# The second half of the adaLN product moves from TensorE to GpSimd

## What is computed

```python
c_act = jax.nn.silu(c)
mod = (c_act @ ada_w[l] + ada_b[l])[:, None, :]          # ada_w: 1024 x 6144
shift1, scale1, gate1, shift2, scale2, gate2 = jnp.split(mod, 6, axis=-1)
u = x * (1.0 + scale1) + shift1
q, k, v, lru_x, lru_gate, gate_a, gate_b = jnp.split(u @ w_in[l], split_at, axis=-1)
...                                                       # attention, RG-LRU, gates -> y
x = _layer_norm(ALPHA * x + gate1 * (y @ w_out[l]), ln1_g[l], ln1_b[l])
u = x * (1.0 + scale2) + shift2
f = _grouped_moe(u, router_w, router_b, moe_w_gate[l], moe_w_up[l], moe_w_down[l])
x = _layer_norm(ALPHA * x + gate2 * f, ln2_g[l], ln2_b[l])
```

## Time and profile before

| | |
|---|---|
| median of three runs | 703.65 us (700.12 to 706.14) |
| profiled execution, time | 704.6 us |
| profiled execution, span of its instructions | 702.8 us |
| mean granted TensorE clock | 0.972 |
| busy: PE, DVE, ACT, POOL | 643.3, 386.0, 221.7, 77.7 us |
| instructions | 15620 |

### The profile page before, as it was taken

One profiled execution on the slowest core, in us unless ns is written; L12 is line 12 of the kernel. 1 busy time (PEld: TensorE's weight loads), 2 busy tenths in 40 slices (PEclk: granted clock), 3 DMA queues, 4 the chain that ended last, 5 costly groups with the idle time before them and its releaser, 6 DMA issues.

```text
span 702.8 us, 15620 instructions
## 1 busy us (share of the span) xinstructions
PE 643.3 (92%) x6021; PEld 433.1 (62%) x6022; DVE 386.0 (55%) x769; ACT 221.7 (32%) x452; POOL 77.7 (11%) x135
## 2 busy tenths in 40 slices
PE   3889999999999899999999956779999999999884
PEld 0377565677777777777778744445555555556363
DVE  0182544367689886466657548653444334433356
ACT  0162533377855565455540142000000000000031
POOL 0032001000000000000000001211122112221400
PEclk9999999999999999999999956999999999999998
DMA  9979976532245342222489794999999999999942
GB/s 322 376 233 329 308 243 216 205 94 87 62 150 165 129 148 81 70 61 91 134 320 419 260 412 162 379 418 398 376 420 417 420 420 417 421 420 420 415 174 120
DMA packets 83070, 188.20 MB, mean 268 GB/s; under 512 B 7084, under 2 KB 59404, under 8 KB 67672
## 3 DMA queue, kind: packets, MB, share of 16 engines
q1 hardware_dynamic: 67808, 148.72, 56.4%
q0 software_dynamic: 7184, 31.74, 12.2%
q10 hardware_dynamic: 8040, 7.23, 3.0%
HBM read 174.12 MB, written 13.54 MB: 267 GB/s over the span
## 4 chain that ended last, share of the span: by engine, by line
PE 78%; DVE 8%; issue 5%; ACT 5%; DMA 3%; SPq 0%; DVEq 0%; ACTq 0%; PEldq 0%
PE psum L1666 22%; PE psum L1676 10%; PE psum L1466 9%; PE psum L1467 8%; PE psum L1468 8%; DMA ada<-in_ada_w_dram 3%; PE psum L1423 3%; PE psum L1587 2%; PE psum L1588 2%; PE psum L1589 2%; PE psum L1712 2%; PE psum L1509 1%; PE psum L1537 1%; PE psum L1547 1%; PE psum L1521 1%
## 5 line engine op out<-in xcount | busy, mean ns | idle before, releaser
L1666 PE MATMUL psum<-wu,xs 128*32 128x256 f32 x1280 | 151.1, 384 | 5.2 <-issue 5.1
L1466 PE MATMUL psum<-uh,whi 128*128 128x512 f32 x336 | 137.7, 410 | 0.0
L1467 PE MATMUL psum<-ul,whi 128*128 128x512 f32 x336 | 131.6, 392 | 0.0
L1468 PE MATMUL psum<-uh,wlo 128*128 128x512 f32 x336 | 131.5, 391 | 0.0
L1666 PE MATMUL psum<-wg,xs 128*32 128x256 f32 x864 | 99.1, 380 | 5.9 <-issue 3.4
L957 DVE TENSOR_TENSOR wlo<-raw,whi 128x1024 fp32r<-128x1024 f32 x42 | 51.3, 1223 | 65.1 <-ACT whi L690 64.8
L882 ACT ACTIVATE hsil<-psum 64x256 f32<-64x256 f32 x40 | 15.0, 376 | 225.7 <-PE psum L1666 225.7
L1283 DVE STREAM_TRANSPOSE xs<-xring 128x256 f32<-128x256 f32 x40 | 26.3, 658 | 106.3 <-PE psum L1666 106.2
L1666 PEld LDWEIGHTS psum<-wg,xs 128*32 128x32 f32 x864 | 51.6, 110 | 47.2 <-issue 18.3
L1676 PE MATMUL psum<-wd,hT 128*32 128x256 f32 x1280 | 78.5, 379 | 2.1 <-DVE hT L1321 1.1
L1666 PEld LDWEIGHTS psum<-wu,xs 128*32 128x32 f32 x1280 | 72.3, 111 | 10.8 <-issue 10.1
(11 more groups left out here) (285 smaller groups left out, 807.0 us busy)
## 6 DMA issues: line engine op xcount, KB each, us to landing
wu<-in_moe_w_up_dram SPq DMA_DIRECT2D x32, 1024.0 KB
wd<-in_moe_w_down_dram SPq DMA_DIRECT2D x32, 1024.0 KB
wg<-in_moe_w_gate_dram SPq DMA_DIRECT2D x22, 1024.0 KB
raw<-in_w_in_dram SPq DMA_DIRECT2D x42, 512.0 KB, 4.1
ada<-in_ada_w_dram POOLq DMA_DIRECT2D x16, 1024.0 KB, 6.7
wg_later<-in_moe_w_gate_dram SPq DMA_DIRECT2D x10, 1024.0 KB
ada<-in_ada_w_dram SPq DMA_DIRECT2D x8, 1024.0 KB, 15.2
y_d<-ysb ACTq DMA_DIRECT2D x144, 32.0 KB
```

Of the source, the lines that this page charges most:

```text
L1466: mmul(bank[s % 2], h[:, k, :], uh[:, k, :], start=(k == 0), stop=False)
L1467: mmul(bank[s % 2], h[:, k, :], ul[:, k, :], start=False, stop=False)
L1468: ins = mmul(bank[s % 2], l[:, k, :], uh[:, k, :], start=False, stop=(k == KT - 1))
L1666: ins = mmul(psum[32 * g:32 * g + 32, 0, 0:256].rearrange("p (a m) -> p a m", a=2), xs[:, k, :], w[:, g % 2], start=(k == 0), stop=(k == K ...
```

## The change

The 4096 columns of the second half are cut into 32 pieces of 128 x 1024 (512 KB), four for each of the eight sets of rows. GpSimd loads them into three buffers of half the former size, multiplies each with its column of silu(c) and adds it to a sum `part2` (128 x 4096) in SBUF. That is one instruction for each of the first four pieces and two for each of the other 28: 60 in all. It does this at steps 1 to 16 (20 pieces) and 25 to 33 (12 pieces), each released by `proj_ps`, the count of finished tiles. After tile 34 and after tile 35 PE adds up the 128 partitions by four products with ones each, in bank 7, and DVE's seven instructions follow at its steps 35 and 36. GpSimd, and no longer SyncE, stores the eight rows to `mod_d`; the waits in SyncE's queue are gone. The loads of `adab2` and `ln1row` move to steps 31 and 32, `zrow` is zeroed first of all, and its nine stores stand behind the pieces of the same step.

```diff
-NA2 = 16
+NA2 = 32
 A2_BUFS = 3
-A2_AT = [3 + (10 * n) // NA2 for n in range(NA2)]
+A2_STEP = [1 + (4 * n) // 5 for n in range(20)] + [25 + (3 * n) // 4 for n in range(12)]
+MOD2_STEP = 34
...
                 if t == START[4] - 3:
-                    sp.wait_ge(S["mod2_row"], 2)
                     load_bias(1)
...
-                if t == 17:
-                    for h in range(2):
-                        sp.wait_ge(S["mod2_row"], h + 1)
-                        for g in range(4):
-                            sp.dma_start(mod_d[h, g:g + 1, :], mod2row[32 * g:32 * g + 1, h, :]).then_inc(mod2_out, 16)
...
+            def load_ada2(n):
+
+                if n >= A2_BUFS:
+                    pool.wait_ge(S["ada2_used"], 2 * (n - A2_BUFS + 1))
+                if n < NA2:
+                    pool.dma_start(ada2[n % A2_BUFS][:, :], ada_v[:, n // 4, (2 + n % 4) * D:(3 + n % 4) * D])\
+                        .then_inc(ada2_sem[n % A2_BUFS], 16)
...
+            def add_ada2(n):
+
+                j, q = n // 4, n % 4
+                w = ada2[n % A2_BUFS][:, :]
+                v = part2[:, q // 2, 2 * (q % 2):2 * (q % 2) + 2, :].rearrange("p g n -> p (g n)")
+                pool.wait_ge(ada2_sem[n % A2_BUFS], 16 * (n // A2_BUFS + 1))
+                if j == 0:
+                    nc.gpsimd.tensor_scalar(v, w, cact[:, j:j + 1], None, ALU.mult).then_inc(S["ada2_used"], 2)
+                else:
+                    nc.gpsimd.tensor_scalar(w, w, cact[:, j:j + 1], None, ALU.mult).then_inc(S["ada2_used"], 1)
+                    pool.wait_ge(S["ada2_used"], 2 * n + 1)
+                    nc.gpsimd.tensor_tensor(v, v, w, ALU.add).then_inc(S["ada2_used"], 1)
...
+            for s in range(1, MOD2_STEP):
+                pool.wait_ge(S["proj_ps"], s)
+                for n in range(NA2):
+                    if A2_STEP[n] == s:
+                        add_ada2(n)
+                        load_ada2(n + A2_BUFS)
...
+            pool.wait_ge(S["mod2_row"], 2)
+            for h in range(2):
+                for g in range(4):
+                    pool.dma_start(mod_d[h, g:g + 1, :], mod2row[32 * g:32 * g + 1, h, :]).then_inc(mod2_out, 16)
...
+            def modulate_sums(h):
+
+                if h == 0:
+                    pe.wait_ge(S["ada2_used"], 2 * NA2)
+                    pe.wait_ge(S["ti_done"], KT)
+                else:
+                    pe.wait_ge(S["mod2_raw"], 1)
+                for g in range(4):
+                    r = 32 * ((g + 2 * h) % 4)
+                    ins = mmul(bank[7][r:r + 32, :], ones[:, 0:32], part2[:, h, g, :], start=True, stop=True)
+                ins.then_inc(S["mod1_ps"], 1)
...
             for s in range(NPROJ):
                 project(s)
-                for n in range(NA2):
-                    if A2_AT[n] == s:
-                        pe.wait_ge(ada2_sem[n % A2_BUFS], 16 * (n // A2_BUFS + 1))
-                        modulate(n // 2, ada2[n % A2_BUFS], bank[2 + n % 2], S["ada2_used"], 2 * (n % 2))
+                if s in (MOD2_STEP, MOD2_STEP + 1):
+                    modulate_sums(s - MOD2_STEP)
...
-                    if n == 0:
-                        pe.wait_ge(S["mod2_raw"], 2)
```

More of the change, by code:

```diff
@@ L591, in _ @@
                                            ada_b[0, lo_:lo_ + 512].partition_broadcast(32)).then_inc(late_in, 16)
+                elif n == NA2 + 1:
                     for h, v in enumerate((ln1_g, ln1_b)):
@@ L604, in _ @@
+            pool.wait_ge(S["c_done"], 1)
+            for n in range(A2_BUFS):
+                load_ada2(n)
+            pool.dma_start(rw[:, :, 0:NE], router_w.rearrange("(k p) e -> p k e", p=P)).then_inc(late_in, 16)
+            pool.dma_start(rbr[:, :], router_b.rearrange("(a e) -> a e", a=1)).then_inc(late_in, 16)
             pool.memset(zrow[:, :], 0.0).then_inc(S["z_done"], 1)
             pool.wait_ge(S["z_done"], 1)
-            pool.wait_ge(mod2_out, 16 * 8)
-            for n, first in enumerate(ZERO_FROM):
-                pool.wait_ge(S["proj_ps"], ZERO_AT + n)
-                blocks_ = min(4, NBLK + 4 - first)
-                pool.dma_start(y_d[first * SUB:(first + blocks_) * SUB, :], zrow[0:blocks_ * SUB, :]).then_inc(S["y_zero"], 16)
+            for s in range(1, MOD2_STEP):
[4 more added lines that the diff above has]
+                        load_ada2(n + A2_BUFS)
+                n = s - ZERO_AT
+                if 0 <= n < len(ZERO_FROM):
+                    first = ZERO_FROM[n]
+                    blocks_ = min(4, NBLK + 4 - first)
+                    pool.dma_start(y_d[first * SUB:(first + blocks_) * SUB, :], zrow[0:blocks_ * SUB, :]).then_inc(S["y_zero"], 16)
@@ L1013, in _ @@
             for s in range(NPROJ + 2):
-                if s == A2_AT[-1] + 1:
-                    dve.wait_ge(S["ada2_used"], NA2)
+                if s == MOD2_STEP + 1:
+                    dve.wait_ge(S["mod1_ps"], 10)
                     dve.wait_ge(late_in, 16 * 14)
-                    for h in range(2):
-                        V.tensor_tensor(mod2row[:, h, :], bank[2 + h], adab2[:, h, :], ALU.add).then_inc(S["mod2_raw"], 1)
+                    V.tensor_tensor(mod2row[:, 0, :], bank[7], adab2[:, 0, :], ALU.add).then_inc(S["mod2_raw"], 1)
+                if s == MOD2_STEP + 2:
+                    dve.wait_ge(S["mod1_ps"], 11)
+                    V.tensor_tensor(mod2row[:, 1, :], bank[7], adab2[:, 1, :], ALU.add).then_inc(S["mod2_raw"], 1)
                     dve.wait_ge(S["mod2_raw"], 2)
@@ L1429, in _ @@
                 pe.wait_ge(ada1_sem[j], 16)
-                modulate(j, ada1[:, j, :], bank[4], S["mod1_ps"])
+                modulate(j, ada1[:, j, :], bank[4])
                 if j == 6:
```

28 lines of the change are left out of this document (10 added, 18 removed).

## The result

The changed kernel takes 730.78 us (median; 721.74 to 736.04, 4 runs) against 703.65 before (four runs too): the ratio is 1.0314, 95% interval 1.0253 to 1.0375. The forecast was 696, faster. The kernel is 3% slower, and the time lies outside the range of 690 to 716.

A forecast was written before the change was run, and what follows sets the result against it. PE was taken to set the time at steps 3 to 12, with DVE and ACT keeping pace around steps 20 to 27. 704.6 - 15.0 + 1.9 + 4.7 = 696.2, say 696 us; range 690 to 716.

The forecast's parts named there:

- Removed and given back: PE loses sixteen pieces' products at tiles 3 to 12, -15.0 us; eight products with ones at tiles 34 and 35, +1.9.
- DVE's seven instructions and the queues: Seven instructions (4.3 us) move from step 13 to 35 and 36; DMA waits, stores and loads move between queues: no cost.
- GpSimd's own time: Per piece, scaling 0.96 us and sum 1.9, so 2.9 us; 93 us of 250, hidden behind PE if it disturbs nobody.
- The middle way: DVE stands still for GpSimd, whose time first fills DVE's idle time and PSUM or one-tile instructions; +4.7 us, steps 25 to 28.
- Rival 1: DVE collides with GpSimd nearly every time: 13.6 us at steps 4 to 12, 10.5 at 25 to 28; 715.6 us, chance 0.28.
- 4 us of room: Steps 4 to 12: second sigmoid ready about 3.4 us after a tile's end, of 7.35; slack of 4 us, once.
- Its ring: Steps 4 to 12: ACT's `xpad`, sigmoid and `whi`, then DVE's `wlo`, `ix` and convolution; 7.2 us against PE's 7.35 a tile.
- Rival 3: GpSimd late at tile 34 if a piece exceeds 4.8 us; 8 us at 5.5 a piece, 703 us with some contention; chance 0.10.
- D: Theory set up for the experiments, not in the prediction: the granted clock of 0.94 costs the time by itself.

The follow-up runs named there:

- e1: Changed kernel without GpSimd's scaling and sum of the 28 pieces after the first four; 705.91 us, ratio 1.0049 to the kernel before; tiles 4 to 40 take 272.6 us.
- e8: Changed kernel with DVE multiplying and adding the pieces in single instructions, at steps 1 to 16 and 29 to 34; 686.17 us, ratio 0.9866 to the kernel before.
- e9: Changed kernel with DVE multiplying and adding the pieces in single instructions, at the change's own steps; 683.29 us, ratio 0.9833 to the kernel before.
- m1: Separate small kernel, not the layer: DVE runs six 128x512 instructions beside one GpSimd 128x1024, all kinds paired; a GpSimd sum held a two-input DVE instruction 2.0 us.
- e2: Changed kernel with the 28 GpSimd scalings but without the 28 sums; 710.46 us, ratio 1.0092 to the kernel before; tiles 4 to 40 take 274.9 us.
- e3: Changed kernel with the 28 GpSimd sums but without the 28 scalings; 747.07 us, ratio 1.0631 to the kernel before; tiles 4 to 40 take 305.3 us.
- e4: Changed kernel with five GpSimd fills in place of each of the 28 pieces' scaling and sum; one execution, 717.2 us; tiles 4 to 40 take 282.0 us.
- e11: Changed kernel with PE's two sets of products with ones a tile later, at tiles 35 and 36; 723.98 us, ratio 1.0404 to the kernel before.

## Why the prediction was wrong, step by step

- **Removed and given back (-15.0, +1.9): right, a little too small.** With GpSimd's arithmetic out (e1) tiles 4 to 40 are 12.6 us shorter than before. My terms give 11.2 for this stretch (15.0 less the two pieces of tile 3, 1.9, less the 1.9 given back). Tiles 4 to 12 lose 14.5 us for 14 pieces, 1.04 a piece and not 0.93, and take 66.5 us where I had said 68. I had read 109.09 to 110.95 in the earlier trace rows; from the product before (108.78) to the next tile's first (112.37) it is 3.59, and 1.55 without pieces (135.09 to 136.64 in after), so two pieces cost 2.04. The second half's stage, with the products with ones and DVE's seven instructions beside it, is 49.68 against 47.65: +2.0 for the 1.9.
- **DVE's seven instructions and the queues (0): right.** e1, e8 and e9 have them all moved and show nothing but those 2.0 us.
- **GpSimd's own time: mis-sized.** Scaling 0.96 forecast, 2.85 alone and 3.08 in the kernel; sum 1.9 forecast, 2.35 and 2.52. A piece is 5.6 us of arithmetic and, with its DMA issue (0.61) and the handovers (0.08 and 0.30 in the rows of step 8), some 6.6 us, where I had 2.9 and 0.53. The Trainium skill's figure for the sum (GPSIMD Engine Reference, section 3.1; an estimate of 2.2 us by it) was nearer than my 1.9, and the runs agree with it. I had taken a fill, which reads nothing, as the nearest row for an instruction that reads.
- **The middle way: the step that failed.** It let GpSimd's time fall first into DVE's idle time, and so gave zero to steps 4 to 16. But GpSimd's pieces do not choose: they are released by the end of a tile, and so is the convolution, which DVE then has to do before ACT and PE can go on. Measured: +14.0 us for tiles 4 to 12, +7.4 for 13 to 16, +14.0 for 25 to 28 (4.7 forecast). What reads PSUM or is a reduction did stay free, as I had assumed (m1). But I had also set all instructions that read only one tile among the free ones, and that is wrong for scalings: in m1 one of 0.49 us takes 2.44 beside a sum, in the kernel 7 of the 8 of L1096 are lengthened, and `ssb<-ssb,rden` by 11.9 us in sum.
- **Even with the right durations the middle way would have failed.** In e2 and e3 it would put nearly the same price on tiles 4 to 12, but e2's GpSimd time in the first stage (40.0 us) is more than the 32 that I had, and costs 0.2 us, while e3's 38.0 us cost 15. It is not GpSimd's time against DVE's idle time that decides, but which instruction of one is under which of the other.
- **Rival 1 had the mechanism** and, for steps 4 to 12, the price: 13.6 worked out, 14.0 measured. That the two agree so closely is in part luck. It put the push at 1.6 us a piece with 4 us of room; DVE's instructions became 22.1 us longer there (58.2 less e1's 36.1), 2.0 a piece, and of the 14.0 only 8.8 are PE's idle time, the other 5.3 are products at the lower clock, which it had not counted. Its ring is what the chain shows (L1099, `wlo`, `whi`, L1096), and PE waits at L1582 (L1547 before) as it said. At steps 25 to 28 it had 10.5 for 14.0, and it left out steps 13 to 16 (7.4), 17 to 24 (2.0, behind a last sum that ends at 176.5 us; not looked into) and the sums at tile 34. Its 715.6 is 15 us under the result, 24.1 us of cost where 43.5 were measured. The rule of the Trainium skill behind it (SBUF — State Buffer, "Who interferes with whom") holds word for word for the sums (held for the sum's whole length) and for PSUM inputs (unaffected), and for DVE's own scalings and copies beside a sum (2.44 us each). For GpSimd's scalings the runs show a hold of 0.7 to 0.8 us in place of 3.
- **Rival 3 came on top.** GpSimd is late at tile 34 (3.7 us of PE's wait, last stage +5.2 over e1), since a piece does take more than the 4.8 us from which I had said that it is.
- **Clock: an effect, and a third of the price.** In tiles 4 to 12 the clock granted to PE is 0.94 in after and e3, and 1.00 (2.4 GHz) in e1, e2, e4 and e9, which run the same products with the same loads. So the new order by itself does not lower it; it is lower in the runs and stages in which PE waits. The timeline of PE in after shows one such place, and under it the same pair of products where PE had not waited:

```profile
87.34 2.05 PE L1582 MATMUL psum<-xc,wax 128*128 128x512 f32 x2 [3.15 <-ACT ix L792]
89.18 1.91 PE L1583 MATMUL psum<-xc,wax 128*128 128x512 f32 x2
90.11 1.42 PE L1505 MATMUL psum<-uh,whi 128*128 128x512 f32 x1
91.31 0.63 PE L1506 MATMUL psum<-ul,whi 128*128 128x512 f32 x1
...
135.32 1.02 PE L1582 MATMUL psum<-xc,wax 128*128 128x512 f32 x2
136.18 1.02 PE L1583 MATMUL psum<-xc,wax 128*128 128x512 f32 x2
136.64 0.79 PE L1505 MATMUL psum<-uh,whi 128*128 128x512 f32 x1
137.27 0.40 PE L1506 MATMUL psum<-ul,whi 128*128 128x512 f32 x1
```

  After 3.15 us of waiting everything runs at about half speed. The granted clock is 1.00 from 78.17 to 83.80 us and 0.50, the lower level of 1.2 GHz, from 87.34 to 93.45; in the second place it is 1.00: from L1582 to the fourth product behind L1506 it takes 6.1 us, until 93.45, in place of 3.1, from 135.32 until 138.43. PE's busy time over tiles 4 to 40 is 282.8 us in after and 268.6 in e1, for the same instructions, and its idle time 33.3 and 4.0. Of the 43.5 us, 29.3 are thus idle time and 14.2 are PE at the lower clock. D falls as a first cause. My forecast and all rivals left this second payment out.

The sum, then: -12.6 + 43.5 = +30.9 over tiles 4 to 40, of which sums that hold DVE are the bulk (32.7 us alone in e3).

**Open:** how the remaining 11 us divide between scalings that push the sums to worse places and GpSimd's lateness; e11 gives some 2.7 to the latter. Nor did a run keep the clock up while PE waited, so how much of the 14.2 us would only turn into longer waits is not known. Why tile 4 begins 3 us earlier in some runs than in others (62.0 in after and e1, 64.1 in e9 and 67.1 in e4, 65.1 in before) was not looked into.

## What to carry to other kernels

Before work is moved to an engine that looks idle, ask which instructions of the bounding ring it will lie beside and what releases it: a helper released by the same event as the ring can collide every time, whatever the idle share of the stage (here each of the eight convolutions was hit, while DVE had been idle for half of the stage before). Compare the helper's hold with the price of doing the work on the busy engine itself: here one DVE instruction of 1.28 us did what cost DVE over 2 us by standing still for GpSimd's two. Price an instruction by a row of its own kind (GpSimd's copy reads as much as its scaling and takes 1.04 us for 2.85), and let an unknown duration pass through every rival, not only the one that it is named in.

## What the runs showed of the hardware that was not expected

- GpSimd's scaling by a value per partition (128x1024) takes 2.85 us, more than its sum of two tiles (2.35) and its copy (1.04) or fill (0.95). Yet it holds a two-input DVE instruction for 0.8 us only, about as long as the copy does, and a later one of the kind not at all; a DVE scaling or copy is held for 0.7 to 0.8 us twice. Why is open.
- A fill (0.95 us) leaves DVE's two-input instructions alone but holds a scaling from SBUF to SBUF by 0.8 us: in e4 the convolution's first instruction went from a mean of 683 ns (e1) to 936, and its other three stayed at 752. In e1 that mean holds one instruction of 1.64 us beside a first piece; the other seven take 0.55.
- GpSimd itself is lengthened by DVE too: the sum by 0.45 us and the scaling likewise (3.30 for 2.85) when a two-input DVE instruction had started 0.07 to 0.10 us earlier. It is the same exclusion from the other side.
- A GpSimd sum of 256 columns takes 0.90 us, of 1024 columns 2.5: the fixed part is some 0.37 us by these two, an estimate ((4 × 0.90 - 2.5) / 3), and it makes cutting up dear.
- Leaving out work that changes values can change the amount of work elsewhere (44 blocks for 40), or its time at equal blocks (378.5 us behind tile 41 in e3, 367.5 in e1), so the totals of such a kernel are not to be compared, only stages ahead of the place where the values act.
